# Order of the twelve down-projection jobs, and who issues the moves of one output tile, in a one-core hybrid decoder step

## The reference

```python
f_gate, f_up = jnp.split(jnp.einsum("btd,df->btf", h2, w_up), [D_FF], axis=-1)
f_conv, new_f = _causal_dwconv(f_gate, buf_f, conv_f_w)
x = x + jnp.einsum("btf,fd->btd", jax.nn.silu(f_conv) * f_up, w_down)   # down projection
...
y = _rmsnorm(x, g_final)      # y = x / sqrt(mean(x*x) + eps) * g_final
```

## Time and profile before

| | us |
|---|---|
| three runs | 854.34, 855.83, 858.22 (median 855.83) |
| profiled execution | 857.45 |
| span in its profile | 855.7 |
| PE busy in the span | 833.3 (97%) |
| DVE / ACT / POOL busy | 715.8 / 431.3 / 144.9 |

### The profile page before, as it was taken

How to read it: one execution, slowest core, us unless ns; L and a number is a source line. 1 busy time by engine, 2 the same in 40 slices (tenths; PEclk the granted TensorE clock), 3 DMA queues, 4 the chain that set the end, 5 groups by cost and what they waited for, 6 DMA issues and landing times. The chain is left out here.

```text
span 855.7 us, 18039 instructions
## 1 busy us (share of the span) xinstructions
PE 833.3 (97%) x6848; PEld 828.7 (97%) x6848; DVE 715.8 (84%) x1078; ACT 431.3 (50%) x782; POOL 144.9 (17%) x114
## 2 busy tenths in 40 slices
PE   8999999999999999999999999999999998999984
PEld 7999999999999999999999999999999998999984
DVE  4899998999999966765679899899999989867744
ACT  7753645364342235762345566466646666434332
POOL 2283838475000000000012200000000016000000
PEclk9999999999999999999999999999999999999997
DMA  9423233432432342319932133423334332435523
GB/s 258 124 82 116 75 98 96 135 101 86 120 101 84 99 109 76 98 49 125 195 100 74 50 99 100 124 74 109 97 95 122 100 92 91 111 94 117 115 56 112
DMA packets 190335, 89.00 MB, mean 104 GB/s; under 512 B 36345, under 2 KB 188813, under 8 KB 190245
## 3 DMA queue, kind: packets, MB, share of 16 engines
q1 hardware_dynamic: 186097, 86.29, 37.9%
q10 hardware_dynamic: 4171, 1.82, 0.8%
HBM read 83.79 MB, written 3.51 MB: 102 GB/s over the span
## 5 line engine op out<-in xcount | busy, mean ns | idle before, releaser
L2114 PE MATMUL psum<-act,w_hi 128*128 128x260 f32 x1984 | 258.6, 283 | 0.0
L2114 PEld LDWEIGHTS psum<-act,w_hi 128*128 128x128 f32 x1984 | 246.3, 188 | 0.0
L2120 PE MATMUL psum<-act,w_lo 128*128 128x260 f32 x992 | 139.9, 283 | 0.0
L1298 DVE TENSOR_TENSOR w_lo<-raw,w_hi 128x1024 fp32r<-128x1024 f32 x78 | 102.0, 1309 | 35.4 <-ACT w_hi L699 35.1
L2120 PEld LDWEIGHTS psum<-act,w_lo 128*128 128x128 f32 x992 | 128.0, 188 | 0.0
L639 POOL TENSOR_TENSOR gate_a<-gate_a,prods 128x512 f32<-128x512 f32 x72 | 109.6, 1523 | 80.8 <-ACT prods L784 72.5
L2284 PE MATMUL psum<-act,w_hi 128*128 128x260 f32 x704 | 112.3, 284 | 0.7 <-ACT tmp L1051 0.7
L1597 DVE TENSOR_TENSOR w_lo<-raw,w_hi 128x1024 fp32r<-128x1024 f32 (+1 forms) x68 | 81.7, 1204 | 23.8 <-ACT w_hi L972 23.7
L2284 PEld LDWEIGHTS psum<-act,w_hi 128*128 128x128 f32 x704 | 97.6, 190 | 0.9 <-ACT tmp L1051 0.9
L699 ACT ACTIVATE w_hi<-raw 128x1024 fp32r<-128x1024 f32 x78 | 82.0, 1053 | 21.6 <-PE psum L2120 16.7
L972 ACT ACTIVATE w_hi<-raw 128x1024 fp32r<-128x1024 f32 (+1 forms) x68 | 69.2, 1027 | 38.5 <-PE psum L2289 26.6
(11 more groups left out here) (264 smaller groups left out, 1251.8 us busy)
## 6 DMA issues: line engine op xcount, KB each, us to landing
raw<-in_w_in SPq DMA_DIRECT2D x56, 512.0 KB, 3.8
raw<-in_w_up SPq DMA_DIRECT2D x44, 512.0 KB, 3.8
raw<-in_w_down SPq DMA_DIRECT2D x16, 448.0 KB, 3.8
v<-in_x_prompt SPq DMA_DIRECT2D x8, 512.0 KB, 7.6
raw<-in_w_b_out SPq DMA_DIRECT2D x8, 512.0 KB, 3.9
raw<-in_w_a_out SPq DMA_DIRECT2D x8, 512.0 KB, 6.0
raw<-in_w_o SPq DMA_DIRECT2D x8, 512.0 KB, 4.2
raw<-in_w_down SPq DMA_DIRECT2D x8, 512.0 KB, 4.6
```

The source lines that it names most:

```text
L1298: ve.tensor_tensor(w_lo[:, slot, 0:k, :], raw[:, s, 0:k, :], w_hi[:, slot, 0:k, :], ALU.subtract).then_inc(lo_done, 1)
L2114: pe.matmul(a[:, h, :], w_hi[:, s, j, :], rhs(k, part)[:, h * H:(h + 1) * H], start=start and part == 0, stop=False)
L2120: last = pe.matmul(a[:, h, :], w_lo[:, s, j, :], rhs(k, 0)[:, h * H:(h + 1) * H], start=False, stop=stop)
```

## The change

The new order is p0 p1 p2 p3 s0 p4 s1 p5 s2 p6 s3 p7. So the first pair job comes one plain job later, p6 comes ahead of s3, and P4 of s3 is issued inside the first part of p7, ahead of its fourth weight tile. The step functions follow: in front of the pairs ACT makes `w_hi` of p1 behind the first of the four token splits instead of the second, DVE makes `w_lo` of p1 ahead of `down_token_lo(0)` instead of behind it, and the splits of the last two groups are spread over p2 and p3. The squares move from ACT's `step_of_s` to `step_of_p`, two tiles ahead of `hi_2`; those of tiles 4 and 5 stand behind s3. The `y_scale` calls come in twos, in steps of s2 and s3 and behind s3. The moves of tile 6, which were all issued by SP, are split: SP issues the first four, ACT the other four (`last_move_y`), ahead of its `hi_up` for p7.

```diff
-    DOWN = [(kind == "s", int(j)) for kind, j in ("p0", "p1", "p2", "s0", "p3", "s1", "p4", "s2", "p5", "s3", "p6", "p7")]
+    DOWN = [(kind == "s", int(j)) for kind, j in ("p0", "p1", "p2", "p3", "s0", "p4", "s1", "p5", "s2", "p6", "s3", "p7")]
...
             for n in range(FT, JOBS):
                 load_down(n)
-                for j in {JOB_P[4]: (0, 1), JOB_P[5]: (2, 3), JOB_P[6]: (4,), JOB_P[7]: (5, 6)}.get(n, ()):
+                for j in {JOB_P[5]: (0,), JOB_S[2]: (1,), JOB_P[6]: (2,), JOB_S[3]: (3,), JOB_P[7]: (4, 5)}.get(n, ()):
                     move_y(j)
+            move_y(KT - 2, range(P // Q // 2))
...
+            def last_move_y(lanes):
+
+                n = KT - 2
+                sc.wait_ge(y_blocked, 2 * n + 2)
+                for a in lanes:
+                    at = slice(P * n + Q * a, P * n + Q * a + Q)
+                    sc.dma_start(y[:, 0:TT, at], y_blocks[n % 2][Q * a:Q * (a + 1), 0:SEQ]).then_inc(y_moved[n % 2], 16)
+                    sc.dma_start(y[0:B, TT, at], y_blocks[n % 2][Q * (a + 1) - B:Q * (a + 1), SEQ:SEQ + Q]).then_inc(y_moved[n % 2], 16)
...
+            def step_of_p(n, squares):
+
+                hi_up(n)
+                for j in squares:
+                    y_square(j)
+                if SEVEN[n + 1]:
+                    hi_2(n + 1)
+                hi_open(n + 1)
...
-            step_of_s(JOB_S[3], (4,))
-            hi_up(JOB_P[6])
-            y_square(5)
-            hi_open(JOB_P[7])
+            step_of_p(JOB_P[6], (2, 3))
+            step_of_s(JOB_S[3])
+            for j in (4, 5):
+                y_square(j)
+            last_move_y(range(P // Q // 2, P // Q))
             hi_up(JOB_P[7])
             y_square(6)
...
             x_times_root(0)
+            lo_open(JOB_P[1])
+            down_token_lo(0)
             x_times_root(1)
-            down_token_lo(0)
-            lo_open(JOB_P[1])
+            lo_up(JOB_P[1])
             plain_out(0)
-            lo_up(JOB_P[1])
...
-            step_of_s(3, (4,))
-            y_block(5)
+            step_of_s(2, (0, 1))
+            step_of_p(3, (4, 5), ())
+            step_of_s(3, (2, 3))
             add_zy(3)
-            lo_up(JOB_P[6])
+            y_block(6)
+            lo_up(JOB_P[7])
             add_21(3)
-            lo_open(JOB_P[7])
+            y_scale(4)
             y_scale(5)
-            plain_out(6)
-            lo_up(JOB_P[7])
-            y_block(6)
...
                     for at in range(KC):
+                        if (part, c, at) == (0, 0, 3):
+                            fourth(JOB_S[KH - 1])
```

More of the change, by code:

```diff
@@ L386, in build @@
         LAST_SEVEN = [max((m for m in range(n) if SEVEN[m]), default=None) for n in range(JOBS)]
-        assert not any(FOLLOWS[FT:]) and not any(SEVEN[-2:])
+        assert not any(FOLLOWS[FT:]) and not SEVEN[-1]
         assert PLAIN[0] == 0 and PLAIN[-1] == FT - 1 and SEVEN[1]
@@ L593, in load_down, with move_y @@
                         sp.dma_start(raw[:, s, 0:KC, :], src).then_inc(raw_in[s], 16)
-            def move_y(n):
+            def move_y(n, lanes=range(P // Q)):
                 par = n % 2
                 sp.wait_ge(y_blocked, 2 * n + 2)
-                for a in range(P // Q):
+                for a in lanes:
                     at = slice(P * n + Q * a, P * n + Q * a + Q)
@@ L1208, in stage_tail_f, with step_of_s @@
                                      f_stage[j][0:n, :]).then_inc(state_out, 16)
[L1210 to L1219, removed]
+            def step_of_p(n, squares):
[5 more added lines that the diff above has]
+                hi_open(n + 1)
+            def step_of_s(n):
                 hi_4(n)
                 up_1(n)
-                for j in squares[:1]:
-                    y_square(j)
                 hi_3(n)
@@ L1228, in step_of_s @@
                 up_5(n)
[L1229 to L1234, removed]
+            down_token_hi(0)
+            hi_open(JOB_P[1])
+            down_token_hi(1)
+            hi_up(JOB_P[1])
             down_token_hi(2)
-            step_of_p(JOB_P[1])
+            hi_open(JOB_P[2])
             stage_tail_f()
             down_token_hi(3)
-            step_of_p(JOB_P[2])
+            step_of_p(JOB_P[2], ())
+            step_of_p(JOB_P[3], ())
             sc.wait_ge(state_out, 16 * 8)
-            step_of_s(JOB_S[0], ())
-            step_of_p(JOB_P[3])
+            step_of_s(JOB_S[0])
+            step_of_p(JOB_P[4], ())
             sc.wait_ge(y_sq_set, 1)
[L1244 to L1247, removed]
-            step_of_s(JOB_S[3], (4,))
-            hi_up(JOB_P[6])
-            y_square(5)
-            hi_open(JOB_P[7])
+            step_of_s(JOB_S[1])
+            step_of_p(JOB_P[5], (0, 1))
+            step_of_s(JOB_S[2])
+            step_of_p(JOB_P[6], (2, 3))
[3 more added lines that the diff above has]
+            last_move_y(range(P // Q // 2, P // Q))
             hi_up(JOB_P[7])
@@ L1899, in ready @@
                 ve.wait_ge(x_by_root, j + 1)
-                if JOB_P[j] < JOB_S[m]:
+                if j < KT - 1:
                     ve.wait_ge(d_out, j + 1)
@@ L1937, in y_block @@
             def y_block(j):
-                if JOB_P[j] < JOB_S[j // 2]:
+                if j % 2:
+                    ve.wait_ge(x_out, j // 2 + 1)
+                    ve.wait_ge(c22_set, NTH[JOB_S[j // 2]] + 1)
+                else:
                     ve.wait_ge(c1_set, NTH[JOB_S[j // 2]] + 1)
-                    ve.wait_ge(x_out, j // 2 + 1)
-                else:
-                    ve.wait_ge(d_out, j + 1)
                 if j > 1:
@@ L1965, in step_of_p @@
                 else:
-                    plain_out(1)
+                    plain_out(2)
                 weight_sum_1(n + 1)
@@ L1977, in step_of_p @@
                 weight_sum_4(n + 1)
+                for j in blocks[1:]:
+                    y_block(j)
                 for j in scales:
                     y_scale(j)
-                for j in blocks[1:]:
-                    y_block(j)
             def step_of_s(m, scales):
                 n = JOB_S[m]
-                plain_out(m + 2)
+                plain_out(m + 3)
                 lo_4(n)
@@ L2462, in _ @@
             down_plain(2)
-            down_seven(0)
             pe.wait_ge(d_out, 2)
             down_plain(3)
-            down_seven(1)
+            down_seven(0)
             pe.wait_ge(d_out, 3)
             down_plain(4)
-            down_seven(2)
+            down_seven(1)
             pe.wait_ge(d_out, 4)
             down_plain(5)
-            down_seven(3)
+            down_seven(2)
             pe.wait_ge(d_out, 6)
             down_plain(6)
+            down_seven(3)
             def turn_last(tiles):
```

17 lines of the change are left out of this document (8 added, 9 removed).

## The result

| | before | after |
|---|---|---|
| median | 856.65 us (4 runs, 854.34 to 858.22) | 844.29 us (4 runs, 843.17 to 844.78) |
| profiled execution | 857.45 | 843.17 |
| span in its profile | 855.7 | 841.4 |
| after / before | | 0.9856, 95% interval 0.983 to 0.9882 |

The kernel is 12.4 us faster by the medians. The forecast was 843.6, with a difference of 12.2; it set out from the median of three runs, 855.83, and the fourth run (857.47) takes the median of before to 856.65.

What follows compares the result with a forecast made beforehand. TensorE was taken as the bound, busy 833.3 of 855.7 us. Stalls -11.86, moved P4 -1.49 and a tail of 23.85 against 22.74 gave -12.2; from the median 855.83 that is 843.6 us, 8-in-10 range 841 to 848.5.

Steps and rivals of the forecast that it cites:

- The stalls, 11.86 us: Time lost in p1, s1, s2, s3 and p6 (4.20, 1.54, 1.57, 4.41, 0.14 us), all expected to go.
- T: Forecast start of p7, 819.6 us: 832.96 less 11.86 and the 1.49 of P4 moved into p7.
- the two causes: DVE's order makes p1's `w_lo` late; ACT's squares ahead of the second PSUM copy make s1 to s3 wait.
- The thin covers: Rival: too little slack in p1 or the pairs, one or two new waits of 1 to 2 us, 846 to 850; chance 0.14.
- the 1.0 us of `lo_up`: Slack in p1: DVE's `lo_up` was to end at 727.4 us, and PE wants it at 728.4.
- the 2.2 of `hi_open`: Slack before the pairs: ACT's `hi_open` ends 9.3 us into the plain job, and PE wants it at 11.54.
- The new wait: In p7, PE waits 2.4 us for `hi_up`, which stands behind ACT's four moves of tile 6.
- The rival of one shared pace: Eight moves on two queues take the same 5.60 us as on one; PE waits 5.2 in p7, 846.4; chance 0.12.
- The clock behind it, 1.8 us: In p7, matmuls behind the 2.4 us wait lose 1.8 us at a lowered clock, taken from p1's similar wait.
- the table: Table of the trace of before by stretches, giving each wait's full price: p1 4.20 us, s1 1.54, s2 1.57, s3 4.41.
- Tail and moved P4: From p7's start to the end: 23.85 us against 22.74 before, of which 1.49 is P4 of s3 moved in.
- the rule of the Trainium skill: A second DMA issuer saves only the initiating, usually little; by it, splitting tile 6's moves brings nothing.

Runs made afterwards that it cites:

- before_p1_first: The kernel before with only p1's weights split earlier, on ACT and DVE, in the old job order: 854.27 us, 0.9972 of before.
- before_squares_last: The kernel before with only both tiles' squares of the pair jobs put behind the three copies out of PSUM: 851.43 us, 0.9946 of before.
- hiup_first: The kernel after with `hi_up` of p7 put ahead of ACT's four moves of tile 6: 841.07 us, 0.9820 of before.
- after_again: The kernel after, unchanged, run once more for a second profile: 844.34 us, span 842.5.
- before_both_spread: The kernel before with p1's weights early, squares behind the copies, and SP issuing one tile's moves at a time: 848.49 us, 0.9903 of before.
- before_both: The kernel before with p1's weights split early and the pair jobs' squares behind the three copies, old job order: 849.44 us, 0.9925 of before.
- additions_first: hiup_first with DVE's last additions for tokens 0 to 255 between the two last multiplications, not behind both: 841.22 us, 0.9826 of before.

## Why the prediction was right, and where it was off

**The stalls, 11.86 us: right.** p1 took 10.15, s1 to s3 8.62 each, p6 (which now carries P4) 11.52, and p7 began at 819.66 where T = 819.6 was forecast. In the timeline of after `lo_open` of p1 starts at 717.38 (forecast 717.4), and ACT's `hi_2` in p6 at 806.66, 7.14 into the job (forecast 7.1). Tile 3's squares there waited less than 0.3 us for their moves. That the two causes were the right ones is shown by before_p1_first and before_squares_last. The thin covers held: the 1.0 us of `lo_up` and the 2.2 of `hi_open` were enough, and P4 in p7 ran without a wait.

**The new wait: right.** Forecast 2.4 us behind ACT's four moves, measured 2.48. ACT's first two issues took 0.76 and 0.88 instead of 0.70, `hi_up` ended at T + 6.58 instead of 6.45. The rival of one shared pace fell: SP's issues stayed at 0.67 beside ACT's. Tile 6 landed at T + 7.3 instead of 6.7, which cost nothing, since PE was last by then.

**The clock behind it, 1.8 us: a toss where the sum had a certainty.** It is 0.1 in the profiled execution (1.99 for fourteen matmuls, 1.86 in hiup_first) and 1.55 in after_again. It was also sized a little high: the 1.8 was all that p1 and s3 lost beyond their waits, but p1 loses 2.70 us with the same wait at full clock (12.75 in before_squares_last, below), so the clock was 1.50 of its 4.20. The profile of after ends 2.1 us before the forecast of 843.5, and this term is most of it. The rest is the end: 6.95 us from the last additions instead of 7.35. In the median the loss is in, and so the median of 844.29 lies near the 843.6.

**The working across executions: a weak step, and luck that it didn't show.** The sum took its stalls from one execution of before in which p1 and s3 both had the clock loss, and took them off a median. The profiled spans differ by 14.3 us, the medians by 12.4, and the forecast had 12.2. Two errors stand against each other. The stalls were priced as that one trace had them: before_p1_first gained 2.2 in the median where the table gives 4.20, and both edits together 7.0 where it gives 11.72. The tail from p7's start, put at 23.85 us, was 21.74 in the trace of after and 23.2 in after_again. So the place of p7 in the trace is a hit of the mechanism (13.30 us earlier as forecast), and the closeness of the medians is in part luck.

**What the order itself brings: hardly in the sum.** Tail and moved P4 come to -0.4 us there, against 4.2 between before_both_spread and after. The prediction had its steps right (tile 6 blocked after s3, moves at 2.6 into p7, last additions close behind PE) but compared them with the tail of before as it was. With the squares behind the copies or in the plain jobs the old order's tail grows from 22.7 to 23.7 and more, which no term foresaw.

**The split: a gain that the sum didn't show.** The sum had tile 6 landing early by it but weighed no kernel without it, nor one with `hi_up` first. As the change stands the gain is eaten by the wait; once `hi_up` stands first it is 1.9 us. The shared-pace rival fell, and the rule of the Trainium skill that the prediction gave it as support gives it none, as said above.

**Shape of the gain.** By medians: p1's weights 2.2, squares out from between the copies 5.0, moves one tile at a time 1.0 (within the spread), the rest of the new order 4.2 (net of the new wait, which costs 3.2; 7.4 without it).

## What to carry to other kernels

Before an engine that also computes issues DMAs, look at what stands behind them on its queue: four issues of about 0.75 us ahead of one weight copy stopped TensorE for 2.5 us, and the copy first cost the DMAs nothing. On a queue that only issues, many small transfers hold up a large load just as well (sixteen moves, 11.6 us), so put them where the next load isn't awaited. When a stall is priced from one trace, look whether its price includes a lowered clock, and compare with more than one execution before taking it off a median.

## What the runs showed of the hardware

- A wait of 2.3 to 2.5 us is followed by matmuls at 1.2 GHz in some executions and not in others. Besides after and after_again, p1 shows it: before took 14.25 us with a granted clock of 0.88, and before_squares_last, with the same wait (2.33), this:

```profile
720.43:733.18 12.75, 10.42 (x87) 10.21 (x85) 12.75 (x22) 4.33 (x11) 4.29 (x5) 1.00 0.31 92
```

The waits of 1.3 us in s1 and s2 didn't show it in the two traces that have them (before, before_p1_first), that of 5.14 did in its one trace. The spread between runs doesn't sort the kernels by it: it is 0.3 us for hiup_first, which has no such wait, and 1.6 for after, which has one, but 3.9 in ten runs of before_p1_first, with one, and 1.9 for before_both, where PE never waits over 0.9 us ahead of its last product.

- At the end of the kernel the stores, not the computing, seem to be the pace: in additions_first the DMA engines are busy for 1.00 of the time from 836 to 837 us, and computing that ends 0.5 us sooner than in hiup_first brings nothing.

- ACT's issuing of a DMA ran beside a computation of ACT that stood ahead of it in program order (822.19 and 822.16 in hiup_first), but a computation behind it waited for the issues to end (825.29 behind 825.19 in after).
